# A two-block model on one core: 104 tokens by gathered rows, the second layer's memory keys and values in front of the experts, and the mixing stage by token tile

## The reference, cut to what matters

```python
q = (ht @ w_q).reshape(T, PEER_HEADS, PEER_QDIM)
s1, s2 = q[..., :128] @ sub_k1, q[..., 128:] @ sub_k2     # scores over 128 keys each
...                                                       # top 16 of each, then top 16 of the 256 sums
gates = softmax(vals)
a = einsum('cd,chkd->chk', xc, expert_u[ec])              # one dot product for each pair
w = gelu(a) * gates
out = einsum('chk,chkd->cd', w, expert_v[ec])             # one weighted row for each pair
```

```python
u, v = gelu(x @ w_in[:, :512]), gelu(x @ w_in[:, 512:1024])   # u * (sgu_w @ layer_norm(v) + b)
p = causal running means of x @ w_in[:, 1024:1536]
mix = concat(gated, pooled) @ w_out
```

## Time and profile before

| | before |
|---|---|
| median of 3 runs | 1845.58 us (1845.53 to 1853.45) |
| profiled execution, its own time | 1852.31 us |
| its span (first to last instruction) | 1850.4 us |
| TensorE busy | 1813.8 us (98%) |
| VectorE busy | 1005.4 us (54%) |
| ScalarE, GpSimd busy | 258.1 us, 257.5 us |
| mean granted TensorE clock | 0.994 of full |
| moved by DMA | 421.71 MB |

### The profile page before, as it was taken

How to read it: one execution, slowest core, us unless ns; L and a number is a source line. 1 busy time by engine, 2 the same in 40 slices (tenths; PEclk the granted TensorE clock), 3 DMA queues, 4 the chain that set the end, 5 groups by cost and what they waited for, 6 DMA issues and landing times.

```text
span 1850.4 us, 28691 instructions
## 1 busy us (share of the span) xinstructions
PE 1813.8 (98%) x11513; PEld 1523.9 (82%) x11513; DVE 1005.4 (54%) x2215; ACT 258.1 (14%) x604; POOL 257.5 (14%) x250
## 2 busy tenths in 40 slices
PE   8999999999999999999999999999999999999996
PEld 6478575789999999999999965889974987699952
DVE  1420133248884988788744433249984223269974
ACT  1014333013443111000000000201100001111100
POOL 0200000000333444344433200000000000000000
PEclk9999999999999999999999989999999999999998
DMA  7445243243899999899999954355454543354441
GB/s 275 159 137 182 96 161 131 95 179 136 335 362 417 367 372 368 331 363 360 380 417 416 403 215 141 110 195 193 160 177 145 179 160 114 131 188 168 175 168 60
DMA packets 71580, 421.71 MB, mean 228 GB/s; under 512 B 8096, under 2 KB 8096, under 8 KB 32688
## 3 DMA queue, kind: packets, MB, share of 16 engines
q1 hardware_dynamic: 42624, 306.20, 45.5%
q0 software_dynamic: 27984, 110.70, 15.5%
q10 hardware_dynamic: 864, 3.27, 0.5%
HBM read 414.83 MB, written 5.24 MB: 227 GB/s over the span
## 4 chain that ended last, share of the span: by engine, by line
PE 85%; DMA 7%; DVE 5%; issue 1%; ACT 1%; POOL 0%; POOLq 0%; ACTq 0%; DVEq 0%
PE ps L800 15%; PE ps L1016 11%; PE ps L476 10%; PE ps L434 9%; PE ps L518 9%; PE ps L808 8%; DMA arena<-v_rows,sparse_pairs 6%; PE ps L443 5%; PE ps L1037 4%; PE ps L698 3%; PE ps L732 2%; DMA arena<-u_rows,sparse_pairs 1%; PE ps L821 1%; PE ps L899 1%; PE ps L594 1%
## 5 line engine op out<-in xcount | busy, mean ns | idle before, releaser
L800 PE MATMUL ps<-xT,ring 128*128 128x168 f32 x2048 | 297.6, 307 | 0.2 <-ACT arena L1245 0.2
L808 PE MATMUL ps<-arena,ring 128*128 128x168 f32 (+1 forms) x2048 | 297.2, 307 | 0.0
L808 PEld LDWEIGHTS ps<-arena,ring 128*128 128x128 f32 x2048 | 292.3, 190 | 0.5 <-issue 0.5
L800 PEld LDWEIGHTS ps<-xT,ring 128*128 128x128 f32 x2048 | 292.3, 190 | 0.5 <-issue 0.5
L476 PE MATMUL ps<-ring,arena 128*128 128x512 f32 x416 | 181.4, 592 | 0.4 <-ACT arena L1296 0.4
L518 PEld LDWEIGHTS ps<-xT,ring 128*128 128x128 f32 x1536 | 173.4, 192 | 3.0 <-issue 2.9
L518 PE MATMUL ps<-xT,ring 128*128 128x128 f32 x1536 | 174.1, 275 | 0.0
L476 PEld LDWEIGHTS ps<-ring,arena 128*128 128x128 f32 x416 | 78.0, 190 | 93.0 <-issue 92.1
L1775 DVE SCALAR_TENSOR_TENSOR arena<-arena,sparse_dots 128x1024 f32<-128x1024 f32 x88 | 112.9, 1283 | 68.4 <-DMA arena<-v_rows,sparse_pairs 65.6
L434 PE MATMUL ps<-xT,ring 128*128 128x256 f32 x672 | 147.1, 380 | 0.0
L434 PEld LDWEIGHTS ps<-xT,ring 128*128 128x128 f32 x672 | 126.9, 190 | 17.4 <-issue 0.3
(11 more groups left out here) (294 smaller groups left out, 2028.2 us busy)
## 6 DMA issues: line engine op xcount, KB each, us to landing
ring<-stream SPq DMA_DIRECT2D x290, 1024.0 KB, 5.2
arena<-second_params POOLq DMA_DIRECT2D x6, 1024.0 KB, 5.6
kv_scratch<-arena POOLq DMA_DIRECT2D x4, 1024.0 KB, 8.1
arena<-kv_scratch POOLq DMA_DIRECT2D x2, 2048.0 KB, 12.4
arena<-second_params POOLq DMA_DIRECT2D x1, 1536.0 KB, 6.3
arena<-u_rows,sparse_pairs POOLq DMA_INDIRECT x90, 9.5
arena<-v_rows,sparse_pairs POOLq DMA_INDIRECT x90, 9.3
arena<-mem_T ACTq DMA_DIRECT2D x2, 512.0 KB, 7.5
```

Of the source, the lines that this page charges most:

```text
L800: ins = pe.matmul(ps[:, o % 2, 0:DENSE], w[:, (o % 2) * D + k * P:(o % 2) * D + (k + 1) * P], xT[:, k, 0:DENSE], start=(k == 0), stop=(k = ...
L808: ins = pe.matmul(ps[:, 4 + k // 2, c:c + DENSE], w[:, (o % 2) * D + k * P:(o % 2) * D + (k + 1) * P], H[:, n, :], start=False, stop=last, ...
```

## The change

Sixteen more tokens go by rows: `SPARSE_B` is 40, in 3 sets of 40 instead of 5 of 24, so its chunks grow from 26 to 43 and all chunks from 90 to 107. The dense tokens fall from 168 to 152 and the gate groups from 21 to 19. There are 7 row buffers instead of 5, and the counts of dot chunks at each place are larger.

The key and value parts of the second memory layer leave the attention's fills and stand between the last key scores and the first expert block. The attention keeps half a fill in each unit.

The mixer's projections are done by token tile. Tile 0 has only dense tokens; its residual, pooled part, v half and u half come before the fold, and VectorE's last 21 row adds stand behind tile 0's residual. The u half's weights leave the stream: one 2 MB load on ScalarE's queue during the last V blocks (`held`).

```diff
-SPARSE_B = 24
+SPARSE_B = 40
...
-DOTS_ROUTING = 18
-DOTS_FIRST = 34
-ROWS = 5
-U_FIRST = 80
+DOTS_ROUTING = 30
+DOTS_FIRST = 50
+LAST_ADDS = 21
+ROWS = 7
+U_FIRST = 96
...
-            ("v0", 4), ("k1", 4), ("v1", 4), ("merge", 4), ("w_out", 4), ("peer_q", 8), ("peer_u", HALF_BLOCKS), ("peer_v", HALF_BLOCKS),
-            ("ab_pool", 2), ("ab_vu", 4), ("ab_out", 4),
+            ("v0", 4), ("merge", 4), ("w_out", 4), ("peer_q", 8), ("k1", 4), ("v1", 4),
+            ("peer_u", HALF_BLOCKS), ("peer_v", HALF_BLOCKS),
+            ("ab_pool", 2), ("ab_v", 2), ("ab_out", 4),
...
             key_scores(PH - 1)
+            for c in range(4):
+                if c >= 2:
+                    pe.wait_ge(xkv_ready, 8 + c - 1)
+                feature_major(slot("k1", c), 4 + c % 2, memT).then_inc(slot_done, 1)
+            for half in range(2):
+                v1_slots = [slot("v1", 2 * half + kh) for kh in range(2)]
+                for i in range(TT):
...
             down_turn(7, 7, last=True)
+            pos[0] += EXPERT_BLOCKS
...
+            ab_pool(0)
+            ab_v(0)
+            pe.wait_ge(held_in, 16)
+            ab_u(0)
             pe.wait_ge(row_added, CHUNKS)
...
-            ab_half(0)
-            pe.wait_ge(xb_copied, 2)
+            ab_pool(1)
+            ab_v(1)
...
-            ab_half(1)
+            ab_u(1).then_inc(u_psum, 1)
...
-            for i, stop in enumerate((2, 21)):
-                with act.Fori(at, stop) as n:
-                    for b in range(2):
-                        expert_act(n * 2 + b, b, n)
-                at = stop
-                act.wait_ge(gate_shift, i + 1)
-                act.activation(g, g, ACT.Exp).then_inc(gate_exp, 1)
+            at = 12
+            with act.Fori(0, at) as n:
+                for b in range(2):
+                    expert_act(n * 2 + b, b, n)
+            gate_exponentials(1)
+            act.wait_ge(kv1_spilled, 32)
...
+            act.wait_ge(slot_done, HELD_FREE)
+            act.dma_start(held, held_d.rearrange("s p n -> p s n")).then_inc(held_in, 16)
...
-                    best16(range(16), sc[:, i], top_v, ti, 1)
+                    best16(range(16), sc[:, i], top_v, ti, 2)
                     candidates(range(PH))
-                    best16(range(PH), cand, val, pu, 1)
+                    best16(range(PH), cand, val, pu, 2)
                     shift_gates()
-                    pick(i, 0, PH, 2)
+                    pick(i, 0, PH, 3)
...
-                        row_adds(44 * (g + 1) // GROUPS - adds_done[0])
+                        row_adds(48 * (g + 1) // GROUPS - adds_done[0])
...
+            row_adds(CHUNKS - LAST_ADDS - adds_done[0])
...
+            dve.wait_ge(slot_done, START["ab_pool"])
+            for q in range(4):
+                residual(0, q)
             row_adds(CHUNKS - adds_done[0])
```

More of the change, by code:

```diff
@@ L673, in values @@
                 ins.then_inc(y_psum, 1)
-            v_slots = {}
+            fill_slots = {}
             def fill(n):
[L679 to L685, removed]
-                    return
[L687 to L692, removed]
-                if i == 0:
[L694 to L703, removed]
@@ new lines, in fill @@
+                if n < 8:
+                    s, t = n // 2, n % 2
+                    if t == 0:
+                        if s:
+                            pe.wait_ge(mgate_ready, 4 + s)
+                        fill_slots["gate"] = slot("mgate_b", s)
+                    w = fill_slots["gate"]
+                    for k in range(KT):
+                        ins = pe.matmul(ps[:, 6, t * T:(t + 1) * T], w[:, k * 2 * P + t * P:k * 2 * P + (t + 1) * P],
+                                        xT[:, k, :], start=(k == 0), stop=(k == KT - 1))
+                    if t == 1:
+                        ins.then_inc(slot_done, 1)
+                    return
@@ new lines, in fill @@
+                half, i, kh = (n - 8) // 4, n // 2 % 2, n % 2
+                if n == 8:
+                    pe.wait_ge(mgate_ready, 8)
+                elif kh == 0:
+                    pe.wait_ge(xkv_ready, 4 + (n - 8) // 2)
+                if i == 0:
+                    fill_slots[kh] = slot("v0", 2 * half + kh)
+                for k in range(4):
+                    ins = pe.matmul(ps[:, 6, :], memT[:, 4 * kh + k, i * P:(i + 1) * P],
+                                    fill_slots[kh][:, k * 512:(k + 1) * 512],
+                                    start=(kh == 0 and k == 0), stop=(kh == 1 and k == 3))
@@ L784, in _ @@
             key_scores(PH - 1)
+            for c in range(4):
[5 more added lines that the diff above has]
+                for i in range(TT):
+                    pe.wait_ge(xkv_ready, 8 + 4 + 2 * half + i - 1)
+                    for kh in range(2):
+                        for k in range(4):
+                            ins = pe.matmul(ps[:, 4 + i, :], memT[:, 4 * kh + k, i * P:(i + 1) * P],
+                                            v1_slots[kh][:, k * 512:(k + 1) * 512],
+                                            start=(kh == 0 and k == 0), stop=(kh == 1 and k == 3))
+                        if i == 1:
+                            ins.then_inc(slot_done, 1)
+                    if i == 0:
+                        ins.then_inc(v_psum, 1)
             pe.wait_ge(xres_T_ready, 2)
@@ L2178, in _ @@
             inv_root(stat[:, 41:42], stat[:, 40:41], 1, 1.0 / HEAD, NORM_EPS).then_inc(kc_rstd, 1)
-            for n in range(1, 4):
-                spill(n, kv_stage[:, HALF_KV * (n % 2):HALF_KV * (n % 2 + 1)])
+            spill(1, kv_stage[:, HALF_KV:])
             row_inverse(1)
```

165 lines of the change are left out of this document (108 added, 57 removed).

## The result

The changed kernel took 1835.7 us (median of 5, 1834.1 to 1837.2), the kernel before on the same chip 1850.96 (median of 5, 1845.53 to 1853.45). The ratio is 0.992, interval 0.9901 to 0.9939: 0.8% faster. The profiled execution took 1835.7 us with a span of 1833.9, 16.5 us under the 1850.4 of before.

A forecast was written before the change was run, and what follows sets the result against it. It took TensorE to bound all four expert stretches, with DMA nearly full beside it. The terms −53.5 − 2.5 + 6 + 18 + 7 gave −25 us, so 1845.58 became 1820.6, stated as 1821; range 1800 to 1850.

The forecast's parts named there:

- the two waits: After the dense blocks TensorE waits 4 to 26 us for tile 0's residual, then about 7 for the last row add.
- The base: The measured median of the kernel before, 1845.58 us, from which the forecast subtracted 25 us.
- The dense blocks: Expert matmuls of 152 instead of 168 columns save 53.5 us; fewer gate groups save 2.5 us.
- the head start is 57 us: Before the first gates, VectorE's 50 dot chunks against 34 fit, as TensorE does 57 us of moved keys and values.
- Attention: Half fills no longer cover the wait for probabilities in units of the second kind: +6 us, from 0 to 12.
- The wait for the residual: At the end of the dense blocks TensorE waits 4 to 26 us for tile 0's residual; taken as 18.
- Around the fold: From the wait's end through the last u half: 61.1 us against 54.3, about +7, including 7 of waiting for last adds.
- the starved stream: Rival, 0.09: in the first and last expert stretches the weight stream stays at 228 GB/s, halving the dense saving; 1830 us.
- The gates that wait for rows: Rival, 0.20: gated expert stretches can't pass 369 GB/s, so late rows delay gates; 1853 us, or 1865 at 350 GB/s.
- The late second routing: Rival, 0.04: the second tile's gates come past their 14 us margin and stop TensorE; 30 us late gives 1837 us.

The follow-up runs named there:

- rows5: The changed kernel with 5 row buffers instead of 7, chunk counts left as they were: 1851.59 us, ratio 1.0007 against the kernel before.
- early: The changed kernel with more dot chunks in the second tile's routing (40 for 30) and more chunks moved forward behind it: 1836.38 us, ratio 0.9924.
- before-again: The kernel before, unedited, run and profiled once more: 1850.71 us, ratio 1.0007.
- tokens88: The changed kernel with the token count and buffers of before (SPARSE_B 24, 5 buffers) and chunk counts scaled to them: 1855.62 us, ratio 1.0015.
- rows104only: The kernel before with 104 tokens by rows and 7 buffers, without the moves, dot chunk counts unchanged: 1874.54 us, ratio 1.0118.
- tokens96_rows5: The changed kernel with 96 tokens by rows (SPARSE_B 32) and 5 row buffers: 1834.35 us, ratio 0.9918 against the kernel before.
- adds28: The changed kernel with 28 instead of 21 row adds behind tile 0's residual: 1835.71 us, ratio 0.9928 against the kernel before.

## Why the prediction was wrong

The direction and the two waits were right, the size was not: −25 us by the sum, −16.5 measured between the profiled executions, and 1821 forecast against 1835.7. Of the 14.7 us between these two, 5.4 are the base that the forecast was laid on. The others are in the sum: it put at nothing the 3.5 us ahead of the attention and the 3.0 us at the end of the program, and its dense term was 3.1 too large, about the wait of 3.4 us that it left out. Its costs in the attention and around the fold came out 1.3 us smaller than forecast, which gave that much back. This makes 8.3 us; the last 1 us lies between the profiled executions and the medians.

- **The base.** The forecast was laid on the median shown, 1845.58. The kernel before gave medians of 1850.71 to 1852.09 afterwards (5 to 17 runs each), with single runs from 1845.5 to 1858.6. Three runs had drawn two of the lowest. This step failed by 5.4 us of the 14.7. Had I stayed with the profiled execution, as the sum did, 1827.3 would have stood there.
- **The dense blocks.** −53.5 and −2.5 were forecast, −52.9 came. The instruction costs 132.6 and 131.6 ns, where the two slopes gave 131.9 to 132.5. Missing is the wait of 3.4 us for the selected gates. The step that failed is "In the first, 50 dot chunks have to be done against 34, but the head start is 57 us", which gave no time for it. The first gather was issued 25.5 us after the first expert block before (474.68 and 449.18 us) and 27.5 us ahead of it now (430.62 and 458.09), 53 us sooner. But 16 chunks at the 3.23 us of the forecast are 52 us (an estimate), and the blocks alone, by the forecast's 148 and 135, end 13 us sooner too. Keys and values were made at 248 GB/s, since no gather ran in their first half.
- **Attention:** +6 forecast, +5.4 measured in the two profiles of the changed kernel. The waits before the transposes of the second kind are 0.62 us in four units, as worked out, and 0.35 in three; the 2.45 of the last unit stand in the kernel before too. But the other nine profiles with the same attention took +8.0: the waits are the same, and the granted clock of its last 14 us was 0.76 to 0.81, where it was 1.00 in these two. Those 2.6 us are in no sum, and what sets them stays open. The last two such waits on the timeline:

```profile
267.20 0.66 PE L649 MATMUL ps<-small,arena 128*128 128x128 f32 x4 [0.62 <-DVE arena L1638]
...
272.15 1.09 PE L649 MATMUL ps<-small,arena 128*128 128x128 f32 x8 [2.45 <-DVE arena L1638]
```

- **The wait for the residual:** 18 forecast, 17.5 measured, but errors cancel, and the agreement to half a us is luck. TensorE's blocks behind the last gates took 141.2 us and not 132, since the last gates stand four blocks ahead of V block 64 (1088 instructions, not 1024). VectorE's 49 chunks in the same stretch took 156 us (879.4 to 1035.4), near the 158 of no row in hand, where I had taken some. And their pace wasn't one: 3.1 us a chunk up to 961 us, 3.8 from 980 to 1022, when most of `held` comes in beside them, and about 2 in the wait itself, where TensorE frees no slot and rows have 4.35 of the 6.31 MB. Over 105 us rows had 15.22 MB, 145 GB/s and not 162, beside the 2.1 MB of `held`:

```profile
877.29 141.18 PE L835 MATMUL ps<-arena,ring 128*128 128x152 f32 x1088
...
q1 hardware_dynamic: 3640, 26.54, 61.0%
q0 software_dynamic: 4180, 15.22, 36.0%
q10 hardware_dynamic: 272, 2.10, 4.8%
```

- **Around the fold:** 7 + 18 forecast, 24.3 measured; the wait for the last adds was 5.9 us in one execution and 7.4 in the other. From L922 to the fold both take 29.9 us; the wait is the shorter where L922 ran longer at the low clock (10.2 and 8.7 us).
- **Never priced: the two buffers.** The prediction names them only as rows in hand. `rows5` shows 16 us of time on them; without them, and with the counts as they are, the change is worth nothing. They don't explain the miss, since the changed kernel has them.
- **Never priced: the end of the program,** +3.0 us, below.

Of the rivals, the starved stream is refuted: the stream had 26.54 MB in 105 us, 253 GB/s, the figure asked for, while the rows are what is short. The rule of the Trainium skill ("DMA: Bandwidth & Descriptors", Queues, rings and completion order) of turns by packet didn't hold the stream back here. The gates that wait for rows are refuted but for the 3.4 us: 402 and 413 GB/s were moved in the gated stretches, so the 369 and 355 of before were not all that could be had beside VectorE's one-hots. The late second routing didn't come up in the changed kernel, only in `early`. The Trainium skill's 358 GB/s for a core (same page, Specifications; its section Bandwidth has it for both cores of a pair streaming) is below what every expert stretch shows on this one core, 402 to 417.

## What to carry to other kernels

Where two chains end together, taking work from one moves the end only as far as the other allows: look for the split at which both end at once (of the three tried here 96 tokens, not 88 or 104), and move work between their ends before shifting more. Price buffers as you price work: here two of them were worth 16 us, most of it around TensorE's waits. Before you fill a head start, look when its first transfer can be issued at all. Before laying a forecast on a median of three, look how far the runs spread; a term of 5 us that comes from the base is as large as most terms of the sum.

## What the runs showed of the hardware

- From VectorE's last operation to the end of the span nothing differs in the kernels' programs, yet it took 8.7 us in the three profiles with 90 chunks (before, `before-again`, `tokens88`), 9.7 and 9.8 with 96, and 11.5 to 11.7 in those with 107, with five buffers or seven, whole rows or half. `rows104only`, the kernel before with more tokens, took 11.7 too. It goes with the number of gathers (180, 192 and 214), some 0.09 us for each; by what, isn't shown.
- The granted clock fell from full to half (2.4 to 1.2 GHz) after waits of TensorE of 2.2 and 2.3 us ahead of the fold (2.33 before, 2.21 in `tokens96_rows5`, where the fold took 4.66 us). It stayed full after 0.61 to 0.69 us, and after 2.05 us ahead of L922 in `adds28` (7.38 us). The length of the wait alone doesn't decide it: the same 2.45 us at the end of the attention were followed by the full clock in the changed kernel and by 0.58 in `rows5`, and in `tokens88` it fell to 0.68 (1098 to 1103 us) with no wait ahead, behind the fold.
- After the 17.5 us wait L922 took 10.20 us, 7.38 at full clock; the granted clock was 0.50 from 1036 to 1041 us and 0.91 in the next 5. After 17.4 and 17.55 us it took 8.71 and 8.83.
- DMA moved 417, 402, 413 and 417 GB/s in the four expert stretches of the changed kernel, 560 us in all.
